# Gated attention: decay sums as differences of running sums on VectorE, q and k of a level in one tile, ada_w chunks spaced wider

## The reference

```python
log_a = jax.nn.log_sigmoid((p_gk @ gla_gk_w + gla_gk_b)) / 16.0      # per token and key feature
q_i, k_i, v_i, b_i = inp                                             # b = running sum of log_a
diff = b_i[:, :, :, None, :] - b_i[:, :, None, :, :]
w = jnp.exp(jnp.where(causal[:, :, None], diff, -jnp.inf))
att = jnp.einsum('bhid,bhjd,bhijd->bhij', q_i, k_i, w)               # decay per feature d
mod = (c_act @ ada_w[l] + ada_b[l])                                  # 6 x 2048
```

## Time and profile before

| | us |
|---|---|
| median of 3 runs (2765.00 to 2771.01) | 2769.29 |
| the profiled execution | 2770.65 |
| its span, first to last instruction | 2768.8 |
| PE busy | 2617.3 (95%) |
| DVE busy | 1763.9 (64%) |
| ACT busy | 1298.4 (47%) |
| granted TensorE clock, mean | 0.985 |

### The profile page before, as it was taken

One profiled execution on the slowest core, in us unless ns is written; L12 is line 12 of the kernel. 1 busy time (PEld: TensorE's weight loads), 2 busy tenths in 40 slices (PEclk: granted clock), 3 DMA queues, 4 the chain that ended last, 5 costly groups with the idle time before them and its releaser, 6 DMA issues.

```text
span 2768.8 us, 37079 instructions
## 1 busy us (share of the span) xinstructions
PE 2617.3 (95%) x13551; PEld 2260.3 (82%) x13551; DVE 1763.9 (64%) x2473; ACT 1298.4 (47%) x1923; POOL 69.9 (3%) x110
## 2 busy tenths in 40 slices
PE   2898999899999999899999999999999998999998
PEld 2787887788878778788888888888889987988996
DVE  5787776676666665677765555556657555666564
ACT  2334344534555534544443444445655544645553
POOL 0000000000000000000000000002000001100000
PEclk9899999999999999999999999999999999999999
DMA  9875666688656566577776666565555564555464
GB/s 341 275 255 174 189 192 190 216 278 285 210 179 191 180 226 219 190 249 249 253 225 194 184 188 189 179 189 153 175 153 159 166 207 123 165 181 150 137 217 141
DMA packets 350398, 554.88 MB, mean 200 GB/s; under 512 B 25102, under 2 KB 169212, under 8 KB 349580
## 3 DMA queue, kind: packets, MB, share of 16 engines
q1 hardware_dynamic: 344320, 541.79, 61.8%
q0 software_dynamic: 3280, 7.64, 0.9%
q10 hardware_dynamic: 2620, 3.09, 0.3%
HBM read 550.35 MB, written 2.10 MB: 200 GB/s over the span
## 4 chain that ended last, share of the span: by engine, by line
PE 79%; issue 6%; DVE 6%; ACT 4%; POOL 1%; DVEq 0%; POOLq 0%; ACTq 0%
PE gp L787 71%; PE tp L787 6%; PE tp L790 2%; DVE wlo L1768 2%; ACT whi L1196 1%; POOL stat L2426 0%; ACT rv L1196 0%; DVE st L1768 0%; DVE acc L1774 0%; ACT L1196 0%; DVE xs L1768 0%; DVE xs L1774 0%; DVE stat L2064 0%; ACT yj L1196 0%; DVE m L1768 0%
## 5 line engine op out<-in xcount | busy, mean ns | idle before, releaser
L1768 DVE TENSOR_TENSOR wlo<-raw,whi 128x1024 fp32r<-128x1024 f32 (+1 forms) x874 | 993.0, 1151 | 632.6 <-ACT whi L1196 630.4
L1196 ACT ACTIVATE whi<-raw 128x1024 fp32r<-128x1024 f32 (+1 forms) x874 | 857.5, 999 | 586.0 <-PE gp L787 505.4
L787 PE MATMUL gp<-whi,h 128*128 128x512 f32 (+1 forms) x3200 | 956.8, 371 | 11.1 <-DVE wlo L1768 6.0
L787 PEld LDWEIGHTS gp<-whi,h 128*128 128x128 f32 x3200 | 596.2, 189 | 89.0 <-issue 19.5
L787 PE MATMUL gp<-h,whi 128*128 128x512 f32 (+1 forms) x1936 | 603.2, 371 | 23.4 <-DVE wlo L1768 16.6
L787 PE MATMUL gp<-wlo,h 128*128 128x512 f32 (+1 forms) x1600 | 584.4, 365 | 0.0
L787 PE MATMUL gp<-h,wlo 128*128 128x256 f32 x1680 | 474.2, 282 | 0.0
L787 PEld LDWEIGHTS gp<-h,whi 128*128 128x128 f32 x1936 | 353.9, 192 | 92.2 <-issue 25.7
L787 PEld LDWEIGHTS gp<-wlo,h 128*128 128x128 f32 x1600 | 303.0, 189 | 31.9 <-issue 1.4
L787 PEld LDWEIGHTS gp<-h,wlo 128*128 128x128 f32 x1680 | 321.2, 191 | 0.8 <-issue 0.7
L1774 DVE SCALAR_TENSOR_TENSOR acc<-raw,cact,acc 128x512 f32<-128x512 f32 x298 | 223.3, 749 | 11.8 <-DMA raw<-in_ada_w_dram 5.0
(11 more groups left out here) (321 smaller groups left out, 2711.1 us busy)
## 6 DMA issues: line engine op xcount, KB each, us to landing
raw<-in_w_in_dram SPq DMA_DIRECT2D x218, 512.0 KB, 4.5
raw<-in_ffn_w_in_dram SPq DMA_DIRECT2D x176, 512.0 KB, 4.7
raw<-in_ada_w_dram SPq DMA_DIRECT2D x158, 512.0 KB, 4.7
raw<-in_w_in_dram SPq DMA_DIRECT2D x192, 384.0 KB, 3.4
raw<-in_w_out_dram SPq DMA_DIRECT2D x96, 512.0 KB, 4.4
raw<-in_ffn_w_down_dram SPq DMA_DIRECT2D x88, 512.0 KB, 4.3
raw_first<-in_ada_w_dram SPq DMA_DIRECT2D x34, 512.0 KB, 5.5
raw<-in_gla_wo_dram SPq DMA_DIRECT2D x32, 512.0 KB, 5.5
```

Source lines behind the costliest of these rows:

```text
L787: return e.matmul(o, l, r, start=start, stop=stop)
L1196: return e.activation(o, i, f, **kw)
L1768: return e.tensor_tensor(o, a, b, op)
```

## The change

- `gla_exp` on PE is gone. `gla_sum` takes its place: sixteen matmuls in all, in four groups, with one table (running sum within each 64 tokens). ACT copies the results back into `LOGA`, laid out [tile of tokens, feature block and token].
- `gla_exp` is now a part of DVE and ACT. Levels 0 to 5: DVE subtracts from every running sum in a segment the one at the segment's middle, one instruction over 128x1024 into `FF[half]`. Level 6: over the first halves alone (128x512). Level 7: four instructions over 128x256. ACT then takes exp of the second halves (scale 1/16) and of the first halves (scale -1/16) in place, SBUF to SBUF; it waits for the subtraction (`gla_diff_done`).
- `gla_qk`: a query product is wanted only in second halves, a key product only in first halves, so both go into one tile `QK`, two instructions over 512 elements, in runs of m tokens with m between them.
- `FF` has two buffers, one per half. `QT` and `KT` are laid out by token tile.
- Order: level 8 first, then the sums, then 16 rounds of three steps: product, exponential of the next, scores.
- The level table is 64 KB and not 576.
- ada_w jobs 8 to 19 go into one list, placed after three of every seven units through GLA's and MLA's kinds (16 and up only in MLA).

```diff
-    more = [(job, ci) for job in adas[8:16] for ci in range(8)]
-    gate_m = [(job, ci) for job in adas[16:20] for ci in range(8)]
+    more = [(job, ci) for job in adas[8:20] for ci in range(8)]
...
-            if kind in ("q", "k", "v", "g", "cq", "ckv", "ga", "ygla") and more and n % 2:
+            mla = kind in ("uq", "ukv", "gb", "ymla")
+            if more and n % 7 in (1, 3, 5) and (mla or kind in ("q", "k", "v", "g", "cq", "ckv", "ga", "ygla") and more[0][0]["seq"] < 16):
                 units.append(more.pop(0))
-            if kind in ("uq", "ukv", "gb", "ymla") and gate_m and n % 3 == 0:
-                units.append(gate_m.pop(0))
...
     if kind == "gla":
+        steps = [step(("gla_z", (), 0), ("gla_sc", (8, 0), 1), need=[("evac", "q", 1), ("evac", "k", 1)]), step(("gla_sc", (8, 1), 1))]
+        steps += [step(("gla_sum", (p,), 1), need=[("gk", 4)]) for p in range(4)]
+        steps += [idle, step(("gla_exp", GLA_ORDER[0], 0))]
+        for i, x in enumerate(GLA_ORDER):
+            steps += [step(("gla_qk", x, 0)), step(*[("gla_exp", y, 0) for y in GLA_ORDER[i + 1:i + 2]]), step(("gla_sc", x, 1))]
...
-        def gla_exp(us, lv, half):
+        def gla_sum(us, p):
+            (u,) = us
             w.wait_ge(loga_done, 2)
             w.wait_ge(d_lvl, 32)
+            bk = empty(u)
+            for t in range(2):
                 for n in range(2):
+                    last = mm(bk[:, (2 * t + n) * P:(2 * t + n + 1) * P], LOGA[:, t, (2 * p + n) * P:(2 * p + n + 1) * P], LV[:, :], True, True)
...
         def gla_exp(us, lv, half):
...
+                m = 1 << lv
+                f4 = segments(ff, lv)
+                second = segments(sums, lv) if lv == 6 else f4
+                w.wait_ge(gla_diff_done, at("diff", lv, half))
+                fn(f4[:, :, :, m:], second[:, :, :, m:], ACT.Exp, scale=sc).then_inc(gla_exp_done, 1)
+                fn(f4[:, :, :, 0:m], f4[:, :, :, 0:m], ACT.Exp, scale=-sc).then_inc(gla_exp_done, 1)
...
+            if lv < 6:
+                m, s4 = 1 << lv, segments(sums, lv)
+                tt(segments(ff, lv), s4, s4[:, :, :, m - 1:m].broadcast_to([P, 2, 256 // m, 2 * m]), ALU.subtract).then_inc(gla_diff_done, 1)
...
         def gla_qk(us, lv, half):
...
-            tt(QF[:, :, tq], QT[:, fb0:fb0 + 4, tq], FF[:, :, tq], ALU.mult).then_inc(gla_qk_done, 1)
-            tt(KF[:, :, tk], KT[:, fb0:fb0 + 4, tk], FF[:, :, tk], ALU.mult).then_inc(gla_qk_done, 1)
...
+                tt(qk[:, :, :, m:], q4[:, :, :, m:], f4[:, :, :, m:], ALU.mult).then_inc(gla_qk_done, 1)
+                tt(qk[:, :, :, 0:m], k4[:, :, :, 0:m], f4[:, :, :, 0:m], ALU.mult).then_inc(gla_qk_done, 1)
```

More of the change, by code:

```diff
@@ L152 @@
 SEQ_B = (4, 0, 5, 1, 6, 2, 7, 3, 12, 13, 14, 15, 16, 17, 18, 19, 8, 9, 10, 11, 20, 21, 22, 23)
+GLA_ORDER = [(lv, half) for lv in range(8) for half in range(2)]
 OFF2 = {"rq": 0, "rk": 768, "rv": 1536, "rg": 2304, "dq": 3072, "dk": 3584, "dv": 4096, "dg": 4608, "lx": 5120, "lg": 5888}
@@ L272, in make_jobs @@
             n += 1
-    assert not more and not gate_m and not gate_f
+    assert not more and not gate_f
     return jobs, units
@@ L876, in gk_krt @@
             last.then_inc(tp_full[u.b], 1)
-        def gla_exp(us, lv, half):
+        def gla_sum(us, p):
+            (u,) = us
             w.wait_ge(loga_done, 2)
             w.wait_ge(d_lvl, 32)
-            for p, u in enumerate(us):
-                bk = empty(u)
+            bk = empty(u)
+            for t in range(2):
                 for n in range(2):
[L884 to L888, removed]
+                    last = mm(bk[:, (2 * t + n) * P:(2 * t + n + 1) * P], LOGA[:, t, (2 * p + n) * P:(2 * p + n + 1) * P], LV[:, :], True, True)
+            last.then_inc(tp_full[u.b], 1)
         def gla_sc(us, lv, half):
@@ L910, in gla_av @@
             bk, vc = empty(u), slice(h * 512, (h + 1) * 512)
-            for lv in (7, 8):
-                for half in range(2):
-                    taken_dve(first_use("gla_sc", lv, half))
+            for half in range(2):
+                taken_dve(first_use("gla_sc", 7, half))
             (result_dve if h < 3 else result_act)("v", h)
@@ L1178, in pe_program @@
         parts = dict(rows=rows, ada_mod=ada_mod, ada_out=ada_out, fn_T=fn_T, gk_la=gk_la, gk_kr=gk_kr, gk_krt=gk_krt,
-                     gla_exp=gla_exp, gla_sc=gla_sc, gla_av=gla_av, gla_og=gla_og, lat_T=lat_T, pr_qn=pr_qn, pr_kn=pr_kn, pr_rr=pr_rr, pr_sc=pr_sc,
+                     gla_sum=gla_sum, gla_sc=gla_sc, gla_av=gla_av, gla_og=gla_og, lat_T=lat_T, pr_qn=pr_qn, pr_kn=pr_kn, pr_rr=pr_rr, pr_sc=pr_sc,
                      pr_pt=pr_pt, pr_av=pr_av, mt_T=mt_T, f_T=f_T, hx_T=hx_T, le_T=le_T, lx_T=lx_T, lg_T=lg_T, lru_g=lru_g, rp_T=rp_T, rt_S=rt_S,
@@ L1970, in gla_z, with gla_exp, sum_at @@
             e.memset(AT[:, :, :, :], 0.0).then_inc(gla_zero, 1)
+        def gla_exp(us, lv, half):
+            ff, sums = FF[half], LOGA[:, :, half * 512:(half + 1) * 512]
+            first_read()
+            for p in (2 * half, 2 * half + 1):
+                taken_act(first_use("gla_sum", p))
+            if lv < 6:
+                m, s4 = 1 << lv, segments(sums, lv)
+                tt(segments(ff, lv), s4, s4[:, :, :, m - 1:m].broadcast_to([P, 2, 256 // m, 2 * m]), ALU.subtract).then_inc(gla_diff_done, 1)
+            elif lv == 6:
+                s4 = segments(sums, 6)
+                tt(segments(ff, 6)[:, :, :, 0:64], s4[:, :, :, 0:64], s4[:, :, :, 63:64].broadcast_to([P, 2, 4, 64]), ALU.subtract).then_inc(gla_diff_done, 1)
+            else:
+                f4, s4 = segments(ff, 6), segments(sums, 6)
+                def sum_at(t, c):
+                    return s4[:, t, :, c:c + 1].broadcast_to([P, 4, 64])
+                tt(f4[:, 0, :, 0:64], s4[:, 0, :, 0:64], sum_at(0, 63), ALU.subtract).then_inc(dve_self, 1)
+                v = own()
+                tt(f4[:, 0, :, 64:], s4[:, 0, :, 64:], sum_at(0, 127), ALU.subtract).then_inc(gla_diff_done, 1)
+                tt(f4[:, 1, :, 64:], s4[:, 1, :, 64:], sum_at(1, 63), ALU.add).then_inc(gla_diff_done, 1)
+                w.wait_ge(dve_self, v)
+                tt(f4[:, 0, :, 0:64], f4[:, 0, :, 0:64], sum_at(0, 127), ALU.subtract).then_inc(gla_diff_done, 1)
+            note(gla_diff_done, "diff", lv, half)
@@ L1972, in gla_qk @@
         def gla_qk(us, lv, half):
-            fb0, tq, tk = 4 * half, (slice(0, S) if lv < 7 else slice(P, S)), (slice(0, S) if lv < 7 else slice(0, P))
-            for u in uses["gla_exp", lv, half]:
-                taken_act(u)
-            first_read()
+            i = GLA_ORDER.index((lv, half))
+            hc, ff = slice(half * 512, (half + 1) * 512), FF[half]
+            w.wait_ge(gla_exp_done, at("exp", lv, half))
             for name in ("q", "k"):
                 w.wait_ge(gp_dve[job_of[name, half]["no"] % 2], at("gpd", name, half))
-            if (lv, half) != (0, 0):
-                read(first_use("gla_sc", lv - 1 + half, 1 - half))
```

95 lines of the change are left out of this document (52 added, 43 removed).

## The result

| | before | changed |
|---|---|---|
| median of the runs, us | 2769.67 (4 runs, 2765.00 to 2771.01) | 2754.98 (4 runs, 2754.25 to 2756.98) |
| profiled execution, its span | 2770.65, 2768.8 | 2755.32, 2753.4 |
| ratio of the times | | 0.9951, 95% interval 0.9939 to 0.9963 |

The changed kernel is 14.7 us faster (10.2 to 16.9 by the interval). Forecast were 9.1. The time lies inside the range of 2745 to 2773, but at the lower edge of the forecast's own case (2755 to 2764).

A forecast was written before the change was run, and what follows sets the result against it. PE was taken to bound the kernel, busy for 95% of the span. The terms -24.9 - 1.0 + 17.0 - 0.7 + 0.5 = -9.1 us gave 2760 us against the median of 2769.29; range 2745 to 2773.

The forecast's parts named there:

- the forecast's own case: Whole kernel: PE waits 11 to 20 us in the decay sums, time 2755 to 2764 us; chance 0.50.
- The waiting, +17.0: Decay-sum levels: DVE's weight rest waits for ACT's copy behind the exponentials, so PE waits 17.0 us more.
- PE's own work, -24.9: Decay sums: sixteen `gla_exp` groups leave PE (28.5 us), four `gla_sum` groups come (3.6); net -24.9 us.
- The first wait, -1.0: First score group at 275.06 us: PE's 0.98 us wait goes, since level 8's scores need no product; -1.0 us.
- The table, -0.7: Head of the kernel: the smaller level table saves 0 to 1.6 us of load time; half taken, -0.7 us.
- The spread, +0.5: New ada_w spacing: nothing gained at 560 to 680 us, more DVE work in MLA; +0.5 us, bounds -1 and +3.
- The cover holds: Rival, decay-sum levels: PE stays the bound, waiting under 4 us, 2743 to 2747 us; 0.20 including times up to the forecast.
- Eaten whole: Rival, decay-sum levels: PE's gaps lower its clock and adaLN waits add, another 4 to 9 us, 2764 to 2769; chance 0.18.
- Slower, short runs: Rival, levels 0 to 5: products and exponentials over short strided runs cost double per element, 2778 us; chance 0.12.

The follow-up runs named there:

- exp_later: Changed kernel with ACT's exponentials one step later, behind the next unit's weight copy; 2737.53 us, ratio 0.9887 to the kernel before.
- idle_step: Changed kernel with one step without work added at the end of each round; 2745.48 us, ratio 0.9923 to the kernel before.
- spread_only: Kernel before the change with only the new spacing of the ada_w chunks, decay sums still on PE; 2764.86 us, ratio 0.9983.
- extra_loads: Changed kernel with three more 512 KB loads on GpSimd's queue ahead of the small level table; 2755.82 us, ratio 0.9960 to the kernel before.
- old_ada: Changed kernel with the ada_w chunks back at their old spacing (every second unit, every third in MLA); 2770.27 us, ratio 1.0006 to the kernel before.
- two_tiles: Changed kernel with each product again over 1024 elements, into a tile of its own; 2769.56 us, ratio 1.0001 to the kernel before.
- later_two_tiles: exp_later with each product again over 1024 elements, into a tile of its own; 2744.74 us, ratio 0.9919 to the kernel before.
- later_old_ada: exp_later with the ada_w chunks at the old spacing of the kernel before; 2747.92 us, ratio 0.9930 to the kernel before.
- later_old_again: Repeat of later_old_ada, the same program; 2745.44 us, ratio 0.9919 to the kernel before.

## Why the prediction was right, and where not

**The waiting, +17.0.** Right in mechanism and place; in size in part by luck. The excess of each of the 15 rounds over the same round of `exp_later`, from scores to scores, each named by the subtraction that stands in it: levels 0 (second half), 1 and 2 1.82, 0.65, 1.01, 1.93, 1.82; levels 3 and 4 0.12 and three times 0.0; level 5 0.75, 1.24; level 6 0.32, 1.28; level 7 1.80, 4.17. Together 16.9 us. The forecast had 1.78 for a typical set, none in levels 3 and 4, 8.0 for the first run of sets (7.35 measured) and 9.0 for the second (9.56). But 1.84 of the last round is the fall of the clock at 419 us, which the forecast had put at nothing. The waiting proper is 15.1, 1.9 less than forecast, and the clock made it good. Both halves of the mechanism were shown by taking them away, the order in ACT's queue wholly (`exp_later`), the short round in part (`idle_step`).

**PE's own work, -24.9.** Right by the records: 256 of tp<-lv,loga became 32. It is right in time, too. `exp_later` and `spread_only` have the same units, and their distances differ by 28.3 us; 0.9 of it are brackets, and some 2.8 the low clock of `spread_only` behind its wait of 3.32 (0.50 from 490 to 494 us). That leaves 24.6.

**The first wait, -1.0.** Wrong. It is as large as before, 1.01 us, now at the scores of level 0, the first that need a product; DVE's product waits for ACT's exponentials, and ACT loads a table just ahead of them:

```profile
289.48 1.28 ACT L1192 ACT_TABLE_LOAD   x1 [5.48 <-DVE ff L1784]
...
293.37 2.05 PE L787 MATMUL tp<-qk 128*128 128x128 f32 x16 [1.01 <-DVE qk L1784]
```

I had only asked whether level 8 waits, not what the next one needs. Level 0's exponential waits for a subtraction, and that for the sums.

**The table, -0.7.** Wrong; nothing, by `extra_loads` and the 62.79 and 62.78 us of the kernels. I had priced bytes where the head waits for something else; for what, no run here shows.

**The spread, +0.5.** The step that failed, with the largest error: about -5 us stand in its place. I looked for its effect in MLA and at the load on the queues. There it cost nothing to be seen: behind the distance, MLA included, the two spans differ by 0.4 us. The effect lies behind the levels, between 440 and 510 us. Nor is it a term by itself: the spacing was worth 2.9 us of the distance without the rest of the change (`spread_only`) and 15.3 us with it (`old_ada`), since it also sets how many rounds have an adaLN pair in the hole. There the waits of before are 1.09, 2.92 and 3.75 us with the clock at 0.96 and 0.87 from 490 to 510 us; of after they are 1.04 and 4.16 with the clock at 1.00 until the second:

```profile
484.25 1.07 PE L790 MATMUL tp<-cst,stg 128*128 128x128 f32 x8 [1.04 <-ACT stg L1192]
508.72 1.92 PE L790 MATMUL tp<-cst,stg 128*128 128x128 f32 x8 [4.16 <-ACT stg L1192]
```

The wait of 2.92 at 498.60 was in the earlier trace rows, where I used it for what it says on the clock, and did not ask if the change would keep it.

**The account.** Of the 15.4 us between the spans, 14.3 lie in the distance of the table. PE's work and the waiting give -24.9 + 16.9 = -8.0. One adaLN sum fewer stands in it (24 records for 32, -0.95; it comes later). The brackets behind the levels are 2.6 us less, and the clock there gives 1.7 (0.04 and 0.13 of 10 us each). These three are the -5 above; 2.9 of it go with the spacing alone by `spread_only`, and what share the shorter stage has in the rest no run shows. That is -13.2; 1.1 us are not assigned (a wait costs more than its bracket, as seen above, and before had one more). So the 14.7 measured against 9.1 forecast are no confirmation of the sum: two terms of it (-1.0 and -0.7) came out at nothing, and the spread at ten times its size and with the other sign. The other -1.1 are -0.7 ahead of the distance, which is scatter, and -0.4 behind it.

**The rivals.** *The cover holds*: no; it is what `exp_later` makes true, and it came out at 2737, below the 2743 to 2747 given for it, by about the 6 us that the forecast missed behind the levels. *Eaten whole*: not here, but it is `old_ada`: the forecast's count of sets was right for one spacing, and with the other the whole gain goes. The clock fell once in the rounds, at 419 us. *Slower, short runs*: no; the products take 685 ns at runs of 1 and of 64 words, and the subtractions 1218 at levels 0 to 5. The exponentials of levels 0 and 1 take 658 ns for 625, which is 5% and not double. The rule of the Trainium skill on SBUF's 16-byte lines ("SBUF — State Buffer", the note on cachelines) said that such runs go at full speed; the trace agrees for DVE, and for ACT down to runs of four words. Its other rule ("VectorE: DVE Perf Modes", The TRN2 errata), 224 cycles of fixed cost from SBUF against 172 from PSUM, has the right sign: 625 against 598 ns, 0.027 us where the estimate was 0.04.

## What to carry to other kernels

When work moves from the engine that is the bound to others, count their instructions in order around each hand-over, not their busy time: here a round trip from DVE to ACT and back stood ahead of the next weight chunk in both queues, and moving one pair of instructions by one step was worth more than the change itself. Compare the period of such a pattern with that of whatever else shares the queue; two patterns of three steps in phase cost 6 us of waiting in the rounds that three in seven did not, and 8 us more behind them, where an adaLN unit gives a stage its step and PE no work. And when a change moves where chunks stand, go through every wait behind it in the trace, small ones too, and ask of each if it will still be there.

## What the runs showed of the hardware

- Fp32 two-operand instructions on DVE over interleaved runs of 1 to 64 words in SBUF took the same 685 ns per 512 elements as contiguous ones. ACT's exponentials over 512 elements took 658 ns at runs of 1 and 2 words and 625 at longer ones.
- A PE wait shown as 1.35 us cost 1.82 us, and one of 2.22 cost 4.17, since the clock fell to its lower level behind it (0.50 from 421 to 423 us). Waits up to 2.07 us (`two_tiles`, `idle_step`) left it at 1.00, and so did some 1.0 us in most rounds of `old_ada`; but in `later_two_tiles` it fell behind waits of 0.28 and 0.90 us.
- 1.57 MB of loads more on GpSimd's queue delayed nothing on PE, though the DMA engines were busy for 0.95 of the time without them and 0.97 with them.
- The runs reached the transposes of `krs` between 249.97 and 255.14 us, with a granted clock of 0.83 to 0.93 from 90 to 140 us; two executions of one program were 4.0 us apart there (254.76 us with 0.86 in `later_old_ada`, 250.76 with 0.93 in `later_old_again`). Behind that point two executions of one program agreed to 0.1 us over 250. A small effect is better read as a distance between two instructions than from the time.
